# Hybrid diffusion trunk step: attention over one key tile by 1024 queries, softmax sums by a ones matmul

## The reference, cut to what matters

```python
def one_block(qblk):
    s = jnp.einsum('bqgrd,bkgd->bgrqk', qblk, k).astype(jnp.float32) * scale
    p = jax.nn.softmax(s, axis=-1).astype(v.dtype)
    return jnp.einsum('bgrqk,bkgd->bqgrd', p, v)
...
k_a = jnp.concatenate([k_c, k_a], axis=1)
v_a = jnp.concatenate([v_c, v_a], axis=1)
o_a = block_attention(q_a, k_a, v_a, MLA_QK ** -0.5).reshape(b, L, MLA_W) * jax.nn.silu(a_g)
...
o_d = block_attention(q_att, k_att, v_att, GQA_HD ** -0.5).reshape(b, L, GQA_W) * jax.nn.silu(d_g)
```

## Time and profile before

| | |
|---|---|
| median of three runs | 5027.0 us |
| profiled execution | 5023.0 us, span 5021.3 us |
| attention, layer 0 | first fill at 1287.75 us, last output multiply at 2227.26 us |
| attention, layer 1 | first fill at 3762.42 us, last output multiply at 4701.51 us |
| TensorE busy in the span | 4336.2 us (86%), 20526 matmul instructions |
| VectorE busy | 3474.3 us (69%) |
| ScalarE busy | 1373.3 us (27%) |
| mean granted TensorE clock | 0.909 of full speed |

### The profile page before, as it was taken

How to read it: one execution, slowest core, us unless ns; L and a number is a source line. 1 busy time by engine, 2 the same in 40 slices (tenths; PEclk the granted TensorE clock), 3 DMA queues, 4 the chain that set the end, 5 groups by cost and what they waited for, 6 DMA issues and landing times. The chain is left out here.

```text
span 5021.3 us, 65810 instructions
## 1 busy us (share of the span) xinstructions
PE 4336.2 (86%) x20526; PEld 2946.9 (59%) x20526; DVE 3474.3 (69%) x8006; ACT 1373.3 (27%) x2266; POOL 468.9 (9%) x529
## 2 busy tenths in 40 slices
PE   5999999668799999976859999994779999999588
PEld 1777777546455555544647777773545555555376
DVE  1588888757567777755637888886666777777466
ACT  0222222211233344431112222221113333443211
POOL 0011111012100000001211101010220000000022
PEclk7999999857799999987979999996668999999799
DMA  9211111122100111005431111111221011110233
GB/s 329 44 53 47 55 48 53 42 73 61 39 22 22 28 44 28 9 16 189 146 108 50 46 53 48 52 52 45 73 65 33 22 28 27 26 32 6 84 134 117
DMA packets 315950, 307.59 MB, mean 61 GB/s; under 512 B 135080, under 2 KB 274728, under 8 KB 309824
## 3 DMA queue, kind: packets, MB, share of 16 engines
q1 hardware_dynamic: 249888, 278.16, 18.4%
q10 hardware_dynamic: 65824, 26.76, 2.2%
HBM read 202.68 MB, written 102.15 MB: 61 GB/s over the span
## 5 line engine op out<-in xcount | busy, mean ns | idle before, releaser
L853 PE MATMUL proj_b<-w_in_w,proj_hT 128*128 128x256 f32 (+2 forms) x3264 | 923.4, 445 | 103.0 <-issue 36.6
L1817 DVE TENSOR_REDUCE attn_mx<-attn_p 128x1 f32<-128x1024 f32 x512 | 626.1, 1223 | 481.3 <-PE attn_p L1662 479.3
L1798 ACT ACTIVATE attn_Pb<-attn_ST 128x1024 f32<-128x1024 f32 (+1 forms) x576 | 562.9, 977 | 1105.0 <-PE attn_ST L1696 605.1
L853 PEld LDWEIGHTS proj_b<-w_in_w,proj_hT 128*128 128x128 f32 x3264 | 644.3, 199 | 352.1 <-issue 224.3
L691 DVE SCALAR_TENSOR_TENSOR proj_GY<-proj_GW,proj_fw,proj_GY 128x128 f32<-128x128 f32 x1920 | 650.4, 412 | 6.1
L1711 PE MATMUL attn_OT<-attn_Pb,attn_V 128*64 128x512 f32 x2176 | 606.8, 616 | 1.5 <-ACT attn_OTs L1784 1.5
L1860 DVE TENSOR_TENSOR attn_acc<-attn_acc,attn_Pb 128x1024 f32<-128x1024 f32 (+1 forms) x448 | 512.2, 1143 | 29.6 <-ACT attn_Pb L1798 15.6
L862 PEld LDWEIGHTS proj_b<-proj_hT,w_in_w 128*128 128x128 f32 x4352 | 493.7, 192 | 19.8 <-issue 16.4
L862 PE MATMUL proj_b<-proj_hT,w_in_w 128*128 128x128 f32 x4352 | 499.7, 276 | 1.4 <-ACT proj_TX L585 1.4
L1662 PE MATMUL attn_p<-attn_K,attn_Q 96*128 96x512 f32 (+1 forms) x1024 | 353.3, 427 | 33.8 <-DVE attn_mx L1817 31.6
L2072 PE MATMUL out_pY<-out_wh,out_oTh 128*128 128x512 f32 x544 | 227.0, 417 | 24.7 <-issue 24.7
(11 more groups left out here) (339 smaller groups left out, 5766.1 us busy)
## 6 DMA issues: line engine op xcount, KB each, us to landing
mod_w<-in_w_mod SPq DMA_DIRECT2D x16, 1536.0 KB, 11.9
scratch_G<-proj_GT SPq DMA_DIRECT2D x34, 512.0 KB, 2.6
out_G<-scratch_G SPq DMA_DIRECT2D x34, 512.0 KB, 5.0
w_in_w<-in_w_in SPq DMA_DIRECT2D x16, 896.0 KB, 11.1
out_O<-scratch_O SPq DMA_DIRECT2D x34, 384.0 KB, 3.8
proj_xt<-in_x SPq DMA_DIRECT2D x17, 512.0 KB, 3.8
fwd_X<-scratch_XC SPq DMA_DIRECT2D x34, 256.0 KB, 2.9
attn_V<-scratch_V SPq DMA_DIRECT2D x16, 544.0 KB, 4.1
```

The source lines that it names most:

```text
L853: mm = pe.matmul(b[bank][:, at:at + e - a], hT[par][:, c, :], w_at(c)[:, a:e], start=(c == 0), stop=(c == DC - 1))
L1798: act.activation(Pb[p % 3][:, 0:w], ST[pair % 2][:, 0:w], ACT.Exp).then_inc(q["exp_done"], 1)
L1817: ins = dve.tensor_reduce(mx[:, t, w:w + 1], p1[:, :], AX.X, ALU.max)
```

## The change

Attention works in blocks of 1024 queries, 2 per head and 16 per layer, and a step (a unit) is one key tile by 1024 queries, so there are 17 equal steps. `pv` puts query columns 0 to 511 on partitions 0 to 63 of `OT` and 512 to 1023 on partitions 64 to 127, and all 17 key tiles accumulate there. The values of two units are issued together, after every even unit, and there are five `Pb` tiles.

Sixteen wide fills and one of eight narrow matmuls serve a block; the maxima of a block are turned by eight transposes into `p1` and not into `misc`. The adds are 16 per block, all of 1024 columns. `finish` is gone. In its place `denominators` (at unit 2 of the next block) multiplies `acc` by a 128x64 matrix of ones, in two matmuls of 512 columns that stand beside each other, so that every partition of `misc` holds the sum of its query. `normalise` on VectorE (at unit 4) takes the reciprocal of all 128x512 of it and multiplies the copied values. `turn` (at unit 8) transposes the result in four matmuls, and `output` on ScalarE (at unit 10) copies it out. Two stores of 512 rows each follow. The next head's `hi` parts all stand at units 1 to 6 of the head's first block and its `lo` parts at units 6, 9, 12 and 15. The diff, cut to its core:

```diff
@@ -1535,12 +1535,13 @@
 
     NKT = NLAT + 1
     KEYS = NKT * P
-    NB = 4
-    NBLK = NH * NB
-    NPAIR = (NKT + 1) // 2
-    WIDE = NLAT * P // 1024
-    NRED = 4 * WIDE + 1
-    NADD = NPAIR - 1
+    QB = 1024
+    NSB = NH * LAT // QB
+    PER = LAT // QB
+    WIDE = LAT // 1024
+    NT_Q = QB // P
+    NADD = NKT - 1
+    NPB = 5
...
-        Pb = [s.sb(f"Pb{i}", [P, 1024]) for i in range(3)]
-        acc = [s.sb(f"acc{i}", [P, 1024]) for i in range(2)]
+        Pb = [s.sb(f"Pb{i}", [P, QB]) for i in range(NPB)]
+        acc = [s.sb(f"acc{i}", [P, QB]) for i in range(2)]
         OTs = s.sb("OTs", [P, 512])
-        mx = s.sb("mx", [P, 4, WIDE + 1])
-        mtm = s.sb("mtm", [P, 4, RM])
-        mtg = s.sb("mtg", [P, 4, RG])
-        den = s.sb("den", [P, 4])
-        Ost = [s.sb(f"Ost{i}", [P, 4, HD]) for i in range(2)]
-        p1 = s.ps("p1", [P, 1024])
-        ST = [s.ps(f"ST{i}", [P, 1024]) for i in range(2)]
+        rden = s.sb("rden", [P, 512])
+        ON = s.sb("ON", [P, 512])
+        mx = s.sb("mx", [P, NT_Q, WIDE + 1])
+        mtm = s.sb("mtm", [P, NT_Q, RM])
+        mtg = s.sb("mtg", [P, NT_Q, RG])
+        Ost = [s.sb(f"Ost{i}", [P, 4, 2 * HD]) for i in range(2)]
...
+                for half in range(2):
+                    rows = slice(b * QB + half * 512, b * QB + half * 512 + 512)
+                    sp.dma_start(S.O[rows, h * HD:(h + 1) * HD].rearrange("(t p) d -> p t d", p=P),
+                                 Ost[B % 2][:, :, half * HD:(half + 1) * HD]).then_inc(q[f"stored{B % 2}"], 16)
+                if b == 0 and h + 2 < NH:
                     load_kq(h + 2)
...
+                for t in range(NT_Q):
+                    mm = pe.transpose(p1[0:rows, t * P:(t + 1) * P], mt[:, t, :], K.ident[:, :])
+                mm.then_inc(q["mrow_done"], 1)
+
+            def denominators(B):
+
+                pe.wait_ge(q["acc_done"], (B + 1) * NADD + START)
+                if B:
+                    pe.wait_ge(q["o_ready"], B + START)
+                for o in range(2):
+                    mm = pe.matmul(misc[o * HD:(o + 1) * HD, :], K.ones[:, 0:HD], acc[B % 2][:, o * 512:(o + 1) * 512], start=True, stop=True)
+                mm.then_inc(q["den_done"], 1)
+
+            def turn(B):
+
+                pe.wait_ge(q["n_ready"], B + 1 + START)
                 for t in range(4):
-                    mm = pe.transpose(misc[0:rows, t * P:(t + 1) * P], mt[:, t, :], K.ident[:, :])
-                mm.then_inc(q["mrow_done"], 1)
-
-            def finish(B, t):
-
-
-                if t == 0:
-                    pe.wait_ge(q["ot_copied"], B + 1 + START)
-                    pe.wait_ge(q["acc_done"], (B + 1) * NADD + START)
-                at, cols = t * (HD + 1), slice(t * P, (t + 1) * P)
-                pe.matmul(misc[:, at:at + HD], OTs[:, cols], K.ident2[:, :], start=True, stop=True)
-                pe.matmul(misc[:, at + HD:at + HD + 1], acc[B % 2][:, cols], K.ones[:, 0:1], start=True, stop=False)
-                mm = pe.matmul(misc[:, at + HD:at + HD + 1], acc[B % 2][:, 512 + t * P:512 + (t + 1) * P], K.ones[:, 0:1], start=False, stop=True)
-                if t == 3:
-                    mm.then_inc(q["fin_done"], 1)
+                    mm = pe.transpose(misc[:, t * P:(t + 1) * P], ON[:, t * P:(t + 1) * P], K.ident[:, :])
+                mm.then_inc(q["turned"], 1)
...
+            def pv(B, kt):
+                par, unit = B // PER % 2, B * NKT + kt
+                pe.wait_ge(q["exp_done"], unit + 1 + START)
+                if kt == 0 and B:
                     pe.wait_ge(q["ot_copied"], B + START)
                 for o in range(2):
-                    kt = 2 * p + o
-                    if kt < NKT:
-                        mm = pe.matmul(OT[o * HD:(o + 1) * HD, :], V[par][:, kt, :], Pb[p % 3][:, o * 512:(o + 1) * 512],
-                                       start=(kt < 2), stop=(kt >= NKT - 2))
+                    mm = pe.matmul(OT[o * HD:(o + 1) * HD, :], V[par][:, kt, :], Pb[unit % NPB][:, o * 512:(o + 1) * 512],
+                                   start=(kt == 0), stop=(kt == NKT - 1))
                 mm.then_inc(q["pv_done"], 1)
...
+                for u in range(NKT):
+                    if B * NKT + u >= 2:
+
+                        pe.wait_ge(q["exp_done"], B * NKT + u - 1 + START)
+                    if u == 0 and not last:
+                        if b == PER - 1:
                             pe.wait_ge(q["hi_ready"], HI0[h + 2] + START)
                             pe.wait_ge(q["lo_ready"], LO0[h + 2] + START)
                             if h + 1 in (NMLA, NMLA + 1):
                                 pe.wait_ge(q["ones_set"], h + 2 - NMLA + START)
                         fill(B + 1, 0)
-                    for o in range(2):
-                        if 2 * p + o < NKT:
-                            scores(B, 2 * p + o)
-                        if p in (2, 3) and B:
-                            finish(B - 1, 2 * (p - 2) + o)
-                    if p < NPAIR - 1:
-                        if not last:
-                            fill(B + 1, p + 1)
-                    elif not last:
-                        max_row(B + 1)
-                    if p:
-                        pv(B, p - 1)
-                pv(B, NPAIR - 1)
-            pe.wait_ge(q["o_ready"], NBLK - 1 + START)
-            for t in range(4):
-                finish(NBLK - 1, t)
+                    scores(B, u)
+                    if not last:
+                        if u < NKT - 1:
+                            fill(B + 1, u + 1)
+                        else:
+                            max_row(B + 1)
+                    if u == 8 and B:
+                        turn(B - 1)
+                    if u >= 2 and u % 2 == 0:
+                        pv(B, u - 2)
+                        pv(B, u - 1)
+                    if u == 2 and B:
+                        denominators(B - 1)
+                pv(B, NKT - 1)
+            denominators(NSB - 1)
+            turn(NSB - 1)
...
+            def output(B):
+
+                act.wait_ge(q["turned"], B + 1 + START)
+                if B >= 2:
+                    act.wait_ge(q[f"stored{B % 2}"], 32 * (B // 2) + START)
+                act.activation(Ost[B % 2][:, :, :], misc[:, :], ACT.Copy).then_inc(q["o_ready"], 1)
...
+                    if unit >= NPB:
+                        was = divmod(unit - NPB, NKT)
+                        act.wait_ge(q["pv_done"], unit - NPB + 1 + START)
                         act.wait_ge(q["acc_done"], was[0] * NADD + max(was[1], 1) + START)
-                    act.activation(Pb[p % 3][:, 0:w], ST[pair % 2][:, 0:w], ACT.Exp).then_inc(q["exp_done"], 1)
-                    if p == 0 and B:
+                    act.activation(Pb[unit % NPB][:, :], ST[unit % 2][:, :], ACT.Exp).then_inc(q["exp_done"], 1)
+                    if u == 0 and B:
                         copy_ot(B - 1)
-                    if p in (2, 4, 6) and b < 2 and h + 1 < NH:
-                        i = 3 * b + p // 2 - 1
-                        if i < len(hi_parts(h + 1)):
-                            hi(h + 1, i)
-                    if p == NPAIR - 1 and B < NBLK - 1:
+                    if b == 0 and h + 1 < NH and 1 <= u <= len(hi_parts(h + 1)):
+                        hi(h + 1, u - 1)
+                    if u == 10 and B:
+                        output(B - 1)
...
+            def normalise(B):
+
+                dve.wait_ge(q["den_done"], B + 1 + START)
+                dve.reciprocal(rden[:, :], misc[:, :]).then_inc(q["rden_ready"], 1)
...
+                if u == 1:
                     if B >= 2:
-                        dve.wait_ge(q["fin_done"], B - 1 + START)
-                    ins = dve.tensor_tensor(sums[:, :], Pb[0][:, :], pair[:, :], ALU.add)
+                        dve.wait_ge(q["den_done"], B - 1 + START)
+                    ins = dve.tensor_tensor(sums[:, :], Pb[(unit - 1) % NPB][:, :], prob[:, :], ALU.add)
                 else:
-                    w = 1024 if p < NPAIR - 1 else 512
-                    dve.wait_ge(q["acc_done"], B * NADD + p - 1 + START)
-                    ins = dve.tensor_tensor(sums[:, 0:w], sums[:, 0:w], pair[:, 0:w], ALU.add)
+                    dve.wait_ge(q["acc_done"], B * NADD + u - 1 + START)
+                    ins = dve.tensor_tensor(sums[:, :], sums[:, :], prob[:, :], ALU.add)
...
+                for u in range(NKT):
+                    if B < NSB - 1:
+                        if u == 0:
                             reduce(B + 1, 0)
-                        if p < NPAIR - 1:
-                            reduce(B + 1, p + 1)
-                        if p == NPAIR - 2:
+                        if u < NKT - 1:
+                            reduce(B + 1, u + 1)
+                        if u == NKT - 2:
                             maxima(B + 1)
-                    if p >= 2:
-                        add(B, p - 1)
-                    if p == 4 and B:
-                        output(B - 1)
```

(26 more changed lines are left out.)

141 lines of the change are left out of this document (61 added, 80 removed).

## The result

The changed kernel takes 5053.6 us (median of 7 runs, 5047.8 to 5059.0), the kernel before 5027.0 beside it (7 runs, 5009.2 to 5036.4): ratio 1.0058, 95% interval 1.0040 to 1.0076. The forecast was 4992. The profiled execution took 5059.0, with a span of 5057.1; before it was 5023.0.

A forecast was written before the change was run, and what follows sets the result against it. TensorE was taken to bound attention, with VectorE able to hold it up through the single fill tile. From 5023, 63 us gained and 31 lost to the clock gave 4991 profiled, 4992 median; range for 8 in 10: 4935 to 5045.

The forecast's parts named there:

- The stall: At fill 7 of each block: normalise holds VectorE 4.0 us, leaving TensorE empty 2.5 us (MLA) or 3.5 (GQA).
- The paces: Time per 1024-query block in mid-attention: MLA 55.9 us, GQA 53.5; without the stall 53.4 and 50.5.
- The prologue: Ahead of the first block: seventeen fills at a bare 2.54 us instead of nine, with extras +22.2 us a layer.
- The last tail: After the layer's last units: bare reciprocal 3.4, multiply 0.7, transposes 0.7, copy 0.7, waits 0.5 us; last 1024 queries 41.5.
- The clock: Half clock behind each block's stall: 1.0 us lost in MLA, 1.2 in GQA, 31 in all; bounds 0 and 48.
- no gain in the middle: Rival, chance 0.14: in the 30 blocks the fill loop is 0.3 us longer in each second unit; 5027 us.
- the clock stays low: Rival, chance 0.12: after each attention stall TensorE stays at 0.50 for three times 3.4 us; 5103 us.
- cheap reciprocal: Rival, chance 0.06: normalise holds VectorE 1.2 us, not 4.0, so no stall or cold stretch; 4877 us.

The follow-up runs named there:

- narrow sums: Changed kernel with sums as columns from eight one-column matmuls, a reciprocal of 8 columns, and division by VectorE on the way out: 4953.6 us, ratio 0.9856.
- late transposes: Changed kernel with the reciprocal in four pieces at units 4 to 7, transposes at unit 10 instead of 8, copy at 12: 4942.6 us, ratio 0.9839.

## Why the prediction was wrong

By its own sum, 63 gained and 31 lost to the clock, the profiled execution should have become 32 us shorter; it became 36 us longer. Of these 68 us, 38 lie in the attention (19 a layer: a gain of 16 was forecast and 3 were lost) and 30 outside it.

- **The stall: right.** The reciprocal took 3351 ns against 3365 from the line through the earlier trace rows; for 128 columns it took 947. `normalise` held VectorE for 4.1 us (4.0), the idle time was 2.58 and 3.49 (2.5 and 3.5), its releaser the reduce. Fill 7 came 21.99 us after the first fill (21.7). The Trainium skill's repeat count of 8 (page "VectorE: DVE Perf Modes", section "First, the fixed hardware budget") would be an estimated 4.3 us if it meant eight cycles a column. The trace does not agree: the rows give six.
- **The paces: right within 1%.** Without the reciprocal the blocks are 53.64 and 50.98 where the sum has 53.4 and 50.5. The ones matmuls run side by side: 0.96 from their start to the next start, where the sum has 0.86 and 0.11 for the change of shape. The prologue has 48.4 us from first fill to first fill (47.6); block 0 took 54.6 (53.8), the last two with the tail 97.5 (96.2). All these residues go one way and make 8 us a layer. The last tail had reciprocal, multiply, transposes and copy as written, but the transposes ran at half clock (1.11 for 0.66).
- **The clock: the term that was mis-sized.** The forecast took 1.0 us a block in MLA and 1.2 in GQA, "the chance of it included". In this kernel there was next to no chance in it: half clock followed 55 of the 56 stalls in the two profiled executions. An MLA block is 57.94 - 53.64 = 4.30 longer than without the reciprocal; 2.6 of it is the stall, 1.7 the clock. In GQA it is 4.98: 3.1 and 1.9. The one stall without half clock gives the same 1.65 for MLA directly. That is 25 us a layer and not 15: 10 of the missing 19, with 8 in the paces above and 1 in the stall. The 3.40 us of full work at half pace lose 1.7; I had written that number down as the bound and then discounted it.
- **Outside the attention: the step that was missing.** The forecast let all other phases stand as they were. They came out 30 us longer in the profiled execution (24 of it in the projection of layer 1), which is nearly the whole measured difference. The padding shows that this is no consequence of what the change does: 48 instructions without an effect move the same phase by 15 to 24 us, up in one kernel and down in the other. The changed kernel with them is level with the kernel before (-3 to +7 us by its interval), which has a short projection too. Where both are long (the changed kernel, and the kernel before padded) the ratios differ by 0.0015 to 0.0026, 8 to 13 us. Its attentions alone are 6 us longer. So the change itself costs little, 13 us at the most, and most of its measured loss is the clock and the waits of phases that it doesn't touch. The projections were seen in one or two profiled executions of each kernel; the medians of 7 and 10 runs moved as they did. What is shown is that the padding moves VectorE's pauses, and that TensorE's wait for GpSimd goes with the length of the projection in 13 traces. Why VectorE pauses there, and how 4 us of waits become 15 to 24 us by the clock behind the next stall, is not shown: that a stall which comes at another moment is followed by more or less half clock is the likely way, and no run sets that moment alone.

Of the rivals, "no gain in the middle" named the right place for part of it: in GQA, values in twos leave every second fill without cover, and taking this back gave 22 us (with the narrow sums; with the reciprocal in one piece it was used up in MLA). The mechanism of "the clock stays low" came true in part (three of seven GQA stalls had 6.8 us and not 3.4), at a small part of its price; with the values singly it came to the 10.2 us that this rival had assumed, five times in the layer. The "cheap reciprocal" was priced at 114 us below the forecast; taking it away gave 134. The Trainium skill's page "TensorE: Matmul & The Clock Gate", section "HAM oscillation — how this bites in real kernels", with its bursts that each start cold after a wait, described the attention better than my discount of it did: here each of 14 waits of 2.6 to 3.5 us had a half-clock stretch behind it. The waits in its example are longer, 3 to 5 us.

## What to carry to other kernels

An operation on an engine with slack is to be priced by its length in one piece and not by its share: here 107 us of reciprocals on VectorE, idle 29% of the time, cost 134 us, since a single buffer refilled every 2 us stood behind them. Cut in four, with its reader moved two units later, the same work cost 24 us a layer, 49 in all (attention 914.9 against 890.6); the ratios of the whole kernels, 0.9839 and 0.9777, say 31, because the first had a short projection and the second a long one. Price an idle time of over 2 us on TensorE in dense work at its length plus 1.7 us, and treat the second term as likely and not as certain: behind such stalls the traces here show from none to 10.2 us at half clock. And a difference below 0.5% in a kernel whose other phases change their length with the place of the code is not to be read as the worth of an edit: compare the phase that was edited, and try a padded twin of both kernels.

## What the hardware showed

- A reciprocal on VectorE costs some 6.3 ns for each further column (175, 947 and 3351 ns for 4, 128 and 512), a plain operation of 1024 columns 1.22 us in all.
- TensorE's clock fell to 1.2 GHz for 3.4 us or more around most stalls of 2.0 to 3.5 us in full work and behind two of 1.33 us; it stayed at 2.4 GHz around a third one of 1.33, around those of 1.28 to 1.61 in the kernel with the late transposes, and around three of 2.00, 2.92 and 2.93 in the one with all values single.
- In the kernel with narrow sums and GQA values single it also fell with no wait over 0.7 us before it, 2.1 to 3.6 us after the start of eight matmuls of one column.
- VectorE pauses some 0.25 us at fixed instructions, in one kernel 128 records apart, in every iteration of layer 1's projection. 48 memsets of 4 columns in the attention 1300 us earlier moved them, and the time of that projection from 896 to 911 us in one kernel, and from 916 or 920 to 896 in another, by half clock behind the same stalls (3.4 or 6.8 us) and by 4 to 5 us of waits.
